# A feed-forward kernel whose down product moves behind all gate and up products, as seven block products in three passes

## The reference

```
h = layer_norm(x) * (1 + sc1) + sh1
q, k, v, u = split(h @ w_in)                    # differential attention on q, k, v; 2-D Fourier mix of u
x = layer_norm(ALPHA * x + (1 + g1) * (concat(o, f) @ w_out)) * ln1_g + ln1_b
h = layer_norm(x) * (1 + sc2) + sh2
a = silu(h @ w_gate) * (h @ w_up)               # 1024 -> 2816
x = layer_norm(ALPHA * x + (1 + g2) * (a @ w_down)) * ln2_g + ln2_b
```

## Time and profile before

| what | us |
|---|---|
| median of 3 runs | 3000.86 (3000.58 to 3001.89) |
| profiled execution, its span | 3005.0 |
| TensorE busy | 2898.0 |
| VectorE, GpSimd, ScalarE busy | 2145.8, 1392.4, 1275.3 |

### The profile page before, as it was taken

One profiled execution on the slowest core, in us unless ns is written; L12 is line 12 of the kernel. 1 busy time (PEld: TensorE's weight loads), 2 busy tenths in 40 slices (PEclk: granted clock), 3 DMA queues, 4 the chain that ended last, 5 costly groups with the idle time before them and its releaser, 6 DMA issues.

```text
span 3005.0 us, 39372 instructions
## 1 busy us (share of the span) xinstructions
PE 2898.0 (96%) x14244; PEld 2436.5 (81%) x14244; DVE 2145.8 (71%) x3092; ACT 1275.3 (42%) x2287; POOL 1392.4 (46%) x1100
## 2 busy tenths in 40 slices
PE   7999998999999998999899999999999999999997
PEld 3888886666666655888789999989999988999996
DVE  5666665988888864556766666677778666777768
ACT  3111112777777764456533233343333333333324
POOL 0233321011111114567755555575677566666755
PEclk9999999999999998999999999999999999999999
DMA  7344347121312105366532122242322224323323
GB/s 261 117 138 131 116 138 185 36 70 57 83 57 71 50 22 189 131 203 224 193 130 71 57 85 71 78 164 71 127 96 94 92 83 159 105 78 126 99 71 106
DMA packets 194061, 333.02 MB, mean 111 GB/s; under 512 B 15366, under 2 KB 102599, under 8 KB 193866
## 3 DMA queue, kind: packets, MB, share of 16 engines
q1 hardware_dynamic: 193868, 330.49, 34.1%
HBM read 250.72 MB, written 79.71 MB: 110 GB/s over the span
## 4 chain that ended last, share of the span: by engine, by line
PE 51%; DVE 4%; POOL 3%; DVEq 1%; ACT 1%; issue 1%; POOLq 1%; DMA 0%; ACTq 0%; SPq 0%
PE tail_bank L2356 9%; PE tail_bank L2358 9%; PE tail_bank L2357 9%; PE tail_bank L2385 5%; PE tail_bank L2387 5%; PE tail_bank L2386 5%; PE tail_bank L2287 1%; PE tail_bank L2289 1%; PE tail_bank L2288 1%; POOL tail_rounded L2085 1%; PE tail_bank L2236 0%; PE tail_bank L2228 0%; PE tail_bank L2229 0%; DMA tail_plain<-scr_h_d 0%; POOL tail_rounded L2101 0%
## 5 line engine op out<-in xcount | busy, mean ns | idle before, releaser
L2085 POOL TENSOR_TENSOR tail_rounded<-tail_plain,tail_rounded 128x512 fp32r<-128x512 f32 x462 | 654.5, 1438 | 481.4 <-ACT tail_rounded L1852 481.2
L2356 PE MATMUL tail_bank<-tail_rounded 128*128 128x384 f32 x1848 | 620.4, 336 | 14.2 <-DVE tail_rounded L2540 5.4
L2358 PE MATMUL tail_bank<-tail_rounded 128*128 128x384 f32 x1848 | 619.6, 335 | 0.0
L2357 PE MATMUL tail_bank<-tail_rounded 128*128 128x384 f32 x1848 | 619.4, 335 | 0.0
L2550 DVE TENSOR_TENSOR tail_plain<-tail_plain,tail_bank 128x384 f32<-128x384 f32 x462 | 247.4, 548 | 259.4 <-PE tail_bank L2358 189.4
L1852 ACT ACTIVATE tail_rounded<-tail_plain 128x512 fp32r<-128x512 f32 x462 | 271.7, 622 | 368.5 <-DVE tail_plain L2526 180.3
L2356 PEld LDWEIGHTS tail_bank<-tail_rounded 128*128 128x128 f32 x1848 | 348.3, 188 | 18.2 <-issue 16.9
L2357 PEld LDWEIGHTS tail_bank<-tail_rounded 128*128 128x128 f32 x1848 | 348.2, 188 | 1.3
L2358 PEld LDWEIGHTS tail_bank<-tail_rounded 128*128 128x128 f32 x1848 | 348.3, 188 | 0.0
L1154 DVE TENSOR_REDUCE att_peak<-att_sc 128x1 f32<-128x1024 f32 x256 | 312.6, 1221 | 42.7 <-PE att_sc L966 36.0
L2385 PE MATMUL tail_bank<-tail_rounded 128*128 128x512 f32 x792 | 310.2, 392 | 11.9 <-DVE tail_plain L2649 4.8
(11 more groups left out here) (290 smaller groups left out, 5139.5 us busy)
## 6 DMA issues: line engine op xcount, KB each, us to landing
tail_plain<-in_w_gu SPq DMA_DIRECT2D x132, 512.0 KB, 4.9
keep_ahead<-in_w_dn SPq DMA_DIRECT2D x66, 512.0 KB, 6.6
proj_ada<-in_w_ada SPq DMA_DIRECT2D x16, 1024.0 KB, 6.9
held_w_hi<-scr_qs_d SPq DMA_DIRECT2D x128, 128.0 KB, 2.9
scr_h_d<-tail_plain SPq DMA_DIRECT2D x63, 256.0 KB, 4.5
proj_x_in<-in_x SPq DMA_DIRECT2D x18, 512.0 KB, 6.7
scr_att_d<-held_w_hi SPq DMA_DIRECT2D x36, 256.0 KB, 2.9
tail_plain<-in_x SPq DMA_DIRECT2D x18, 512.0 KB, 4.3
```

The lines of the kernel that those rows point to most:

```text
L2085: nc.gpsimd.tensor_tensor(w_lo[:, j, :], operand(F, j), w_hi[:, j, :].bitcast(F32), ALU.subtract).then_inc(wlo_done, 1)
L2356: nc.tensor.matmul(dst, w_hi[:, j, cols], h_hi[j][:, k, :], start=(k == 0), stop=False)
L2357: nc.tensor.matmul(dst, w_hi[:, j, cols], h_lo[j][:, k, :], start=False, stop=False)
L2358: m = nc.tensor.matmul(dst, w_lo[:, j, cols], h_hi[j][:, k, :], start=False, stop=(k == 3))
```

## The change

**The steps.** The 33 steps keep their two phases. `down`, `split_a`, `split_down`, `total` and the norms beside the steps are gone. Each step's activations, four quarter tiles, go to memory (`store_a`, four transfers a step into `scr_a_d`). In the second block VectorE also builds, part by part, the four sums of w_down's 2 x 2 blocks (`turn_down`), which are stored in `scr_dn7_d`. The next block's h is loaded and split earlier (`opens_next`, `closes`), and for that VectorE takes two of three lower halves.

**The down stage.** Behind the last step follow 27 units: 3 passes over the hidden rows (4, 3 and 4 pairs of row blocks, `PASS_PAIRS`), and in each pass 9 pairs of tiles (`QUEUE`). A unit is 7 products of 4 or 3 pairs, three matmuls of 512 columns each. The weights of a pass stay in SBUF, as 28 or 21 pieces of two halves, split at the end of the pass before (`split_piece`). For a unit its activations are loaded (`load_a`), VectorE makes four sums of them (`sums2`), ScalarE and GpSimd split seven operands (`split_a2`), ScalarE copies the first product (`first_of_unit`) and VectorE adds the others up (`take_product`). After passes 0 and 1 the result goes to memory (`store_out`) and comes back in the next pass (`load_back`, `add_back`). In pass 2 both tiles are finished: `final` (stored part, gate, residual) on VectorE, `moments` and `normalise` on ScalarE, `rstd` and `scale` on GpSimd, `shift` on VectorE one unit later, then two stores.

The core of the diff (in the order SP, ScalarE, GpSimd, TensorE, VectorE, memory):

```
+        PASS_PAIRS = (4, 3, 4)
+        FIRST_PAIR = (0, 4, 7)
+        QUEUE = NT // 2
+        UNITS = 3 * QUEUE
...
+            def store_a(G):
+                b, part = divmod(G, PARTS)
+                for n, (i, c) in enumerate(A_ORDER):
+                    sp.wait_ge(mult_done, 4 * G + n + 1)
+                    sp.dma_start(a_d[PAIRS * b:PAIRS * (b + 1), part, :, 2 * c + i, :].rearrange("q p z -> p q z"),
+                                 sils[G % 2][:, i, c, :].rearrange("p (q z) -> p q z", z=P)).then_inc(a_stored[G % 2], 16)
...
+                else:
+                    sp.wait_ge(final_done, 2 * (u - 2 * QUEUE))
+                sp.wait_ge(*stored_by(u - QUEUE))
+                sp.dma_start(back[u % 2 if c == 1 else 0][:].rearrange("p c z -> p (c z)"), out_d[c - 1, q]).then_inc(
+                    back_landed[u % 2 if c == 1 else 0], 16)
+                if c == 2:
+                    for i in range(2):
+                        sp.dma_start(back[1][:, i, :], x1_d[FFN_ORDER[2 * q + i]]).then_inc(back_landed[1], 16)
...
+            def rows_of_the_norm():
+                for m in (len(PIECES) - 1, len(PIECES) - 2):
+                    sp.wait_ge(*piece_low(m))
+                sp.dma_start(gate2, mod_rows[1:2, G2 * D:(G2 + 1) * D].to_broadcast([P, D])).then_inc(row2_landed, 16)
+                sp.dma_start(norm_g, ln2_g.to_broadcast([P, D])).then_inc(row2_landed, 16)
+                sp.dma_start(norm_b, ln2_b.to_broadcast([P, D])).then_inc(row2_landed, 16)
...
+            for u in range(UNITS):
+                if u + 2 < UNITS:
+                    load_a(u + 2)
+                if 0 < u <= 2 * QUEUE:
+                    store_out(u - 1)
+                if QUEUE - 1 <= u < 2 * QUEUE - 1:
+                    load_back(u + 1)
+                if u == 2 * QUEUE:
                     rows_of_the_norm()
+                if u >= 2 * QUEUE:
+                    load_back(u)
...
+            def split_a2(u, p):
+                act.wait_ge(*a2_ready(p, u))
+                act.wait_ge(*a2_free(p, u))
+                nc.scalar.activation(a2(p, u)[0], a2_raw(p, u), ACT.Copy).then_inc(a2hi_done, 1)
+            def first_of_unit(u):
+                act.wait_ge(down_done, OPERANDS * u + 1)
+                if u >= 2:
+                    act.wait_ge(*stored_by(u - 2))
+                else:
+                    act.wait_ge(wlo_done, OPERANDS * PHASES)
+                nc.scalar.activation(outs[u % 2][:, 0, 0, :], out_bank(OPERANDS * u), ACT.Copy).then_inc(first_done, 1)
...
+            for u in range(UNITS):
+                c = pass_of(u)
+                for j in range(OPERANDS):
+                    if j == 0:
+                        first_of_unit(u)
+                    if u + 1 < UNITS:
+                        split_a2(u + 1, j)
+                    if c < 2 and u % QUEUE == QUEUE - 1:
+                        for m in pieces_of(c + 1, j, (0, 1, 2)):
+                            split_piece(m)
+                    if u == QUEUE + 1 + j:
+                        split_piece(piece_at(2, j, 3))
+                    if u > 2 * QUEUE:
+                        if j == 0:
+                            moments(u - 1, 1)
+                        if j == 1:
+                            moments(u - 1, 0)
+                        if j in (2, 3):
+                            normalise(u - 1, 3 - j)
...
+            for u in range(UNITS):
+                c = pass_of(u)
+                for j in range(OPERANDS):
+                    if u + 1 < UNITS:
+                        split_a2(u + 1, j)
+                    if c < 2 and u % QUEUE == QUEUE - 1:
+                        split_piece(piece_at(c + 1, j, 2))
+                    if u == QUEUE + 1 + j:
+                        split_piece(piece_at(2, j, 3))
+                    if u > 2 * QUEUE:
+                        if j in (1, 2):
+                            rstd(u - 1, 2 - j)
                         if j in (3, 4):
...
+                            scale(u - 1, 4 - j)
...
-            def down(G):
...
+            def unit(u):
+                c, n = pass_of(u), pairs_in(u)
+                for p in range(OPERANDS):
+                    at = OPERANDS * u + p
+                    if u % QUEUE == 0:
+                        for t in range(n):
+                            pe.wait_ge(*piece_low(piece_at(c, p, t)))
...
+                        pe.wait_ge(bank_read[at - 4], (1, 2, 2, 1)[at - 4] * PHASES)
+                    else:
+                        v, r = divmod(at - 8, OPERANDS)
+                        pe.wait_ge(*((taken, (OPERANDS - 1) * v + r) if r else (first_done, v + 1)))
+                    dst = out_bank(at)
+                    hi, lo = a2(p, u)
+                    for t in range(n):
+                        w_hi2, w_lo2 = w2(p, t)
+                        nc.tensor.matmul(dst, hi[:, t, :], w_hi2, start=(t == 0), stop=False)
+                        nc.tensor.matmul(dst, hi[:, t, :], w_lo2, start=False, stop=False)
+                        m = nc.tensor.matmul(dst, lo[:, t, :], w_hi2, start=False, stop=(t == n - 1))
+                    m.then_inc(down_done, 1)
             def step(b, part, G):
                 phase(b, part, 2 * G)
-                if part and G < END:
-                    down(G - 1)
                 phase(b, part, 2 * G + 1)
...
+            for u in range(UNITS):
+                unit(u)
...
+            def sums2(u):
...
+                nc.vector.tensor_tensor(s3[:, 0:n], a11, a21, ALU.subtract).then_inc(s_done, 1)
                 dve.drain()
+                nc.vector.tensor_tensor(a21, a21, a22, ALU.add).then_inc(s_done, 1)
                 dve.drain()
+                nc.vector.tensor_tensor(s2[:, 0:n], a21, a11, ALU.subtract).then_inc(s_done, 1)
                 dve.drain()
+                nc.vector.tensor_tensor(s4[:, 0:n], a12, s2[:, 0:n], ALU.subtract).then_inc(s_done, 1)
...
+            def take_product(u, p):
+                tile = outs[u % 2]
+                c11, c12, c21, c22 = (tile[:, c, d, :] for c in range(2) for d in range(2))
+                src = out_bank(OPERANDS * u + p)
+                if p == 1:
+                    dve.wait_ge(first_done, u + 1)
+                dve.wait_ge(down_done, OPERANDS * u + p + 1)
+                if p == 5:
+                    nc.vector.tensor_tensor(c22, c22, src, ALU.add)
+                dst, first = ((c12, c11), (c22, c12), (c11, c11), (c21, c22), (c12, c12), (c12, c12))[p - 1]
+                nc.vector.tensor_tensor(dst, first, src, ALU.add).then_inc(taken, 1)
...
+            def add_back(u, c):
+                if c:
+                    for done in back_ready(u):
+                        dve.wait_ge(*done)
+                tile = out_row(u, c)
+                ins = nc.vector.tensor_tensor(tile, tile, back[u % 2][:, c, :], ALU.add)
...
+            def final(u, c):
+                if c:
+                    for done in back_ready(u):
+                        dve.wait_ge(*done)
+                    dve.wait_ge(row2_landed, 64 if u == UNITS - 1 else 48)
+                tile = out_row(u, c)
+                nc.vector.tensor_tensor(tile, tile, back[0][:, c, :], ALU.add)
                 dve.drain()
+                nc.vector.tensor_tensor(tile, tile, gate2, ALU.mult)
                 dve.drain()
+                nc.vector.scalar_tensor_tensor(tile, back[1][:, c, :], ALPHA, tile, ALU.mult, ALU.add).then_inc(final_done, 1)
+            def shift(u, c):
+                dve.wait_ge(scaled, tile_number(u, c) + 1)
+                tile = out_row(u, c)
+                nc.vector.tensor_tensor(tile, tile, norm_b, ALU.add).then_inc(y_done, 1)
...
+            for u in range(UNITS):
+                c = pass_of(u)
+                if u + 1 < UNITS:
+                    sums2(u + 1)
+                for j in range(OPERANDS):
+                    if j:
+                        take_product(u, j)
+                    if c < 2 and u % QUEUE == QUEUE - 1:
+                        for m in pieces_of(c + 1, j, (0, 1)):
+                            split_piece(m)
+                    if u > 2 * QUEUE and j in (5, 6):
+                        shift(u - 1, 6 - j)
+                    if c and j > 4:
+                        (add_back if c == 1 else final)(u, 6 - j)
...
-    total_d = scratch("scr_total_d", [NT // BLOCK_TILES - 1, BLOCK_TILES, P, D])
+    a_d = scratch("scr_a_d", [NT // 2, FT // 2, P, 4, P])
+    dn7_d = scratch("scr_dn7_d", [FT // 2, 4, P, 512])
+    out_d = scratch("scr_out_d", [2, NT // 2, P, 2 * D])
...
```

894 lines of the change are left out of this document (409 added, 485 removed).

## The result

The changed kernel takes 3051.7 us in the median of four executions (3044.7 to 3057.9), against 3001.4 for the kernel before on the same chip: a ratio of 1.0166, 95% interval 1.0148 to 1.0183, 50 us slower. TensorE has 297 matmuls less and does the rest at the old pitch, so what is lost is lost in its waits and in the lower clock that follows some of them.

The account below looks back on a forecast made before the run. TensorE was taken as the bound before, VectorE/GpSimd turns and work order in the new third pass. Matmuls -67.3, gaps +2, third pass +99 gave a 3038.6 us span, forecast 3034 us, slower; range 2965 to 3065.

Parts of the forecast that it names:

- steps, block ends: Gate and up steps: cost nothing, except 3 us per block end where the hidden state is split.
- entry to the down stage: Start of the down stage: rounding 28 weight and 7 activation pieces on GpSimd and VectorE costs some 7 us.
- changes of pass: The down stage's two changes of pass: GpSimd's 14 splits and VectorE's operations leave about 3 us each.
- Term 1: Down product's matmuls: 2079 instead of 2376 at 0.2267 us each, -67.3 us; units of 19.0 us, 14.3 in pass two.
- Term 2: Gaps that go: stops around the two block ends and about 1.5 us at the first down product, -17 us.
- Term 3: Gaps that come up to the third pass: block ends, down-stage entry and pass changes, +19 us (bounds 0 and 35).
- Cover is thin: Block ends: splits' cover called thin where 12 GpSimd and 10 VectorE splits fall in 14.6 us; 3 us each.
- Term 4: Third pass: VectorE and GpSimd turns plus work order make units 30 us; 287 us instead of 171.4 + 16.7.
- 60 to 70%: Sign in the third pass: TensorE busy about 60 to 70%, stopping for the splits of the activations.
- A: Third pass: turns are cheaper and only the work's order counts, units of 24.7 us, 2992 us; chance 0.20.
- B: Third pass: TensorE stays the bound, helpers' chains hidden, a unit under 19.0 us, 2940 us; chance 0.15.
- C: Entry and pass changes cost more, or TensorE's lower clock joins in the third pass: 3075 to 3100 us; chance 0.07.

Follow-up runs that it names:

- folded: Against the changed kernel, every pass does product x gate + stored part and the first adds alpha x1: 3044.5 us, a unit of 27.2.
- 5 and 10 splits: Against the changed kernel, VectorE takes 5 of the 15 low-half splits in a block's last phase and GpSimd 10, as before the change: 3055.0 us.
- 8 and 7: Against the 2997.3 us version (folded sums except last tile pair, scaling on VectorE, earlier moments), VectorE 8 splits, GpSimd 7, one final operation later: 3002.1 us.
- both orders mended: Against the changed kernel, VectorE's first-pair swap and ScalarE's moments-first order together, clock at 1.00: 3038.3 us, a unit of 27.1.
- first pair swapped: Against the changed kernel, VectorE's final operations on a unit's first tile precede the shift of the previous unit's first tile: 3036.6 us, a unit of 27.7.
- moments first: Against the changed kernel, ScalarE takes the second tile's moments before the next unit's first product, the first tile's behind the first split: 3042.5 us.
- both pairs swapped: Against the changed kernel, VectorE's final operations precede the previous unit's shift for both tiles: 3060.5 us, a unit of 30.9.
- scaling on VectorE: Against the changed kernel, the norm's scaling moves from GpSimd to VectorE, directly ahead of the shift: 3016.4 us, a unit of 24.9.
- scaling of 64 columns: Against the changed kernel, GpSimd multiplies only the first 64 of each row's 1024 columns by the norm's scale: 3012.0 us, a unit of 24.3.
- folded, scaling on VectorE: Against the changed kernel, folded sums, the norm's scaling on VectorE and ScalarE's second-tile moments ahead of the first product: 3009.2 us, a unit of 22.8.
- without the norm: Against the changed kernel, the third pass leaves out gate, residual and norm, only adding the stored part: 2952.8 us, units of 19.0.

## Why the prediction was right, and where it was not

Span 3042.9 measured, 3038.6 forecast. By its own terms:

```
                               forecast   measured
start of gate and up             1446.2     1437.7    -8.5
steps, block ends                  +6        +23.8   +17.8
entry to the down stage            +7        +11.0    +4.0
changes of pass (to 2nd, to 3rd)   3+3        0, and 4.6 inside pass three   -6
third pass, with its tail         287       283.6     -3.4
```

The five differences add to +3.9 against 4.3 in the spans; the rest is rounding.

That the spans come so close is in part luck. In all runs whose time and span are both known the time is 1.7 to 2.1 us above the span, so the trace of before, 3005.0, is of an execution of about 3007 us by my estimate, 6 over its median, while the trace of the changed kernel is the fastest of four. The 8.5 us at the start of gate and up are such a difference between executions (the folded kernel, profiled in one of 3052.7 us, has 1445.3 there) and hide half of what the block ends cost more. Median against median, 3034 was forecast and 3051.7 measured: 17.7 us too little, inside the range of 2965 to 3065.

Term 1 was right: 2079 matmuls, 14.3 and 19.0 us a unit, the old pitch. Term 2 was right on the old stops around the block ends, but the 1.5 us at the first down product were not won: the first three steps lose 25.9 us, the first two before lost 23.0. That loss sits in both kernels, and the forecast carried it over without naming it.

Term 3 is the mis-sized one: block ends 23.8 us, not 6. I had the method and did not use it there. With the prices of the prediction a last phase has 12 GpSimd splits of 1.30, 14 VectorE operations of 0.55 and four multiplications (about 0.45): 25 us of turns in a phase of 14.6, 10 us late, where the ends lost 11.0 and 12.8. "Cover is thin" should have been that sum. The clock's fall behind the stop is inside the measured loss. The sum gives the size and not the order of the three versions: with 5 and 10 splits it gives 14.3 us late (13.0 and 16.0 measured), with 8 and 7 it gives 12.0, more than with 10 and 5, and 9.7 and 11.1 were measured, less. What sets the last us or two there, the order of the work or the clock, stays open.

Term 4 was right in size and in its first cause, the turns. Predicted: unit 30 us between ends of 26 and 33; measured 29.2. First unit's end 41 us into the pass, measured 45.1: the queue issued the rows 20.9 us into the pass instead of 18, and the last x1 tile landed at about 36.8 instead of 32. VectorE waited 9.08 us for it:

```profile
2796.09 1.23 DVE L2739 TENSOR_TENSOR tail_plain<-tail_plain 128x1024 f32<-128x1024 f32 x1 [9.08 <-DMA tail_plain<-scr_x_d]
```

Seven units took 203.7 us instead of 210, the last 21.6 instead of 23, the tail 13.2 instead of 13. TensorE was busy for 78% and not for the 60 to 70% that the prediction named as a sign: at a mean clock of 0.86 its matmuls are recorded longer.

What the prediction had wrong is how the loop closes. It held VectorE's wait for the scaling and the turns to be all; it said of the store, 3.1 us, that it is just in time. The store is a link, as the chain and the swaps show:

```profile
y<-tail_plain SPq DMA_DIRECT2D x18, 512.0 KB, 2.6
```

That the turns set what no order gets under rests on all runs together. The sums are GpSimd's 15.5 us (16.3 with start-up) and VectorE's 10.8 from the prediction, with each edit's own change. Beside them stands what the traces have: the time in which a GpSimd instruction, or a VectorE instruction that does not read PSUM, is recorded as running, overlaps counted once, per unit over four steady units:

```
kernel                     sum of turns   traced   a unit
both orders mended          26.3-27.1      26.1     27.1
first pair swapped          26.3-27.1      26.1     27.7
moments first               26.3-27.1      26.4     28.3
changed kernel              26.3-27.1      26.5     29.2
both pairs swapped          26.3-27.1      26.0     30.9
folded                      24.1-24.9      24.0     27.2
scaling on VectorE          23.7-24.5      23.3     24.9
scaling of 64 columns       22.1-22.9      22.3     24.3
folded, scaling on VectorE  21.5-22.3      21.3     22.8
without the norm               13.5        13.6     19.0
```

No unit is under its sum, and the best order comes to its upper end. The traced time settles what the sums only argue: five kernels with the same work and units from 27.1 to 30.9 us have it at 26.0 to 26.5, and with both orders mended no pause in it is longer than 0.15 us, so there another order of the same instructions has at most 1.0 us left to win. What lies above it is the order's, up to 4.9 us. Without the norm it is 13.6 us, under TensorE's 19.0, and there TensorE sets the unit. A (24.7 from the order alone) and B fall: nothing that computed the whole result came under 22.8, and only leaving the finishing work out gave 19.0. C's price falls, since 3051.7 is not 3075, and its lower clock is not what makes the unit long, by the run that had full clock. A run in which GpSimd's splits of pass three are absent was not made.

The median lies 7 us over the profiled execution. Executions of one kernel are 13 us apart, 14 in the kernel without the norm; the start of gate and up, all code before it being equal, was read between 1437.2 and 1445.3 in thirteen profiles. Where this comes from stays open.

## What to carry to other kernels

Before splitting a stage so that work gathers in its last part, add up per unit of that part what each engine there does, and for VectorE and GpSimd one sum of both, as whole instructions that take turns: 26 us of turns do not hide behind 19 us of matmuls, however much room 62% and 71% busy seemed to leave before. Then follow each in-order queue once round the loop, through the store that frees a buffer. And moving work off the engine that the waits name can lose time if the other one takes longer turns at the same port: five splits moved to GpSimd cost 5 us, two gained 3. Move it to where fewer or shorter turns are taken (the scaling: 2.40 us of GpSimd against 1.08 of VectorE), or out of that part altogether.
